# Second mixer's front: operands of small VectorE instructions moved to PSUM, and GpSimd's low parts of six strips made whole

## The chip, the cores and the metric

The kernel runs on one core of a Trainium2 chip, in one launch. The time is device microseconds of that core; the runs shown agree within 1.2 us. The engines are TensorE (PE; its weight loads are PEld in the profile), VectorE (DVE), ScalarE (ACT), GpSimd (POOL) and SyncE (SP), which issues the DMAs.

## What is computed

The reference is two small transformers in a row, on 256 tokens of width 1024, in float32: two layers of the first kind, then two of the second. The change lies in the second kind, `hybrid_layer`; here is its part that matters:

```python
h = rms_norm(x, ln_mix)
z = h @ w_in                                    # split into n_q, n_kc, ..., m_q, merge
q   = partial_rope(rms_norm(split_heads(q, H), q_norm), positions) * (dh ** -0.5)
k_s = partial_rope(rms_norm(split_heads(k_s, G), k_norm[1]), positions)
k_w = partial_rope(rms_norm(split_heads(k_w, G), k_norm[2]), positions)
...
k, v = jnp.split(rms_norm(mem, mem_norm) @ w_kv, 2, axis=-1)    # memory attention
k = rms_norm(split_heads(k, H), k_norm)
```

`partial_rope` turns the first 16 of a head's 64 values by the angles of the positions: `[x1*cos - x2*sin, x2*cos + x1*sin, rest]`. `rms_norm` divides by the root of the mean square. Behind the mixers of a layer stands an MLP; the first kind of layer has two gated MLPs around a mixer of its own.

## The kernel before

**The stream.** All big weights come as 616 pieces of 128 x 1024 float32, in the order of use, by SyncE's queue into a ring of 7 places. Each piece is multiplied to nearly float32 precision by three fast products. ScalarE rounds the piece (`round_piece`, L1350: `hi`), GpSimd subtracts that from the piece (`pool_program`, L563: `lo`, in the piece's own place), and TensorE multiplies `hi` with the high part of the activations, `lo` with the same, and `hi` with their low part (`product`, L590 to L592). A piece of a strip is 12 matmuls of 512 columns. ScalarE rounds a piece at most 4 ahead of TensorE, in a ring of 5, and waits for `used`, TensorE's count of pieces done.

**GpSimd** does a piece in one instruction in the MLPs and in four (`parts`) in the mixers. Which pieces are in a mixer is told by `in_mixer`. Ahead of a piece in four parts it also waits until its previous piece has ended.

**The second mixer** (`mix2`) works on strips of 512 columns, four pieces each, in the order `nk, nq, z3, mk, mq, mv, gqk, gv`, six of `merge`, `gr`, and then rows of the branches. TensorE puts strips by turns into PSUM banks 0, 1 and 2, 3; ahead of a strip it waits until the strip two before it has been taken out (`evicted`). VectorE takes out `nk`, `z3`, `mv`, `gv` and the merges, ScalarE `mk`, `mq`, `gqk`.

Between the pieces each engine does small steps; their order is written out by hand in `mix2_work`, the same list for all engines. Around the change VectorE's order is this:

- `memory_in` 2: variance and square root of the memory rows (`m_cells`, 2 columns); ScalarE makes a first guess by Ln and Exp, VectorE improves it in four instructions (`rsqrt`, L1857 to L1860).
- `prep` 1: sums of squares of the 24 heads' values (L2199) and their variance (`variance`, L1866), for which ScalarE then waits with its next guess, in front of its next rounding.
- `windows` 0 and 1 (L2183, L2189): windows of keys and values for the compression, from PSUM.
- the taking of `z3` out of PSUM (L2052).
- `prep` 2: square root of the heads (`cells24`, 24 columns; `rsqrt`), then the heads are scaled (L2205).
- `prep` 3: the rotation by the angles (`rotate`, L2163 to L2168), six instructions on 192 columns.
- `mem` 1 and 3: variance and square root of the memory keys (`k_cells`, 8 columns), then the keys are scaled (L2219). TensorE transposes them behind strip `mq` (L812).

All these small instructions have their operands in SBUF; only the windows and the taking read PSUM. Later `nsa_step` 0 (L2346 to L2350) begins the hidden layer of the compression, and `mem_unit` makes the scores of the memory attention (L2236, L2040), which TensorE transposes (L822). L2355 ends the hidden layer's gelu; TensorE waits for it at L1126.

`TURNED` is PSUM bank 6, which TensorE uses for transposes before and behind these steps.

Of the kernel before, what the change touches and what calls it, by code (L numbers as in the profile page):

```python
# [15 lines left out]
ALU = mybir.AluOpType  # L16
# [3 lines left out]
P = 128  # L20
# [270 lines left out]
class Views:  # L291


    def __init__(self, M):
# [3 lines left out]
        def cell(n):  # L298
            at[0] += n
            assert at[0] <= 500, at  # L300
            return small[:, at[0] - n:at[0]]
# [100 lines left out]
        self.tmp_v = self.hid[1][:, 0:64]  # L402
        self.mn16, self.sum16, self.inv16 = cell(16), cell(16), cell(16)
        self.cells24 = (cell(24), cell(24), cell(24))
        self.cells8 = (cell(8), cell(8), cell(8))
        self.m_cells = (cell(2), cell(2), cell(2))
        self.k_cells = (cell(8), cell(8), cell(8))
        self.c_cells = (cell(1), cell(1), cell(1))
        self.dests = {"nk": self.znq[:, :, 512:1024], "nq": self.znq[:, :, 0:512], "mq": self.mq, "z3": self.zz,
                      "gqk": self.gqk, "gv": self.gv, "mk": M.memkv[:, :, 0:512], "mv": M.memkv[:, :, 512:1024]}  # L410
# [130 lines left out]
def in_mixer(c):  # L541

    block, at = divmod(c, PIECES1) if c < L * PIECES1 else divmod(c - L * PIECES1, PIECES2)
    if c < L * PIECES1:
        return FFN_PIECES + 6 <= at < PIECES1 - FFN_PIECES - 4
    return 8 <= at < PIECES2 - 8 * MLP_STRIPS - 4


def pool_program(M, sem):
# [768 lines left out]
def act_program(M, V, sem, landed):  # L1318
# [10 lines left out]
    def own(instruction):  # L1329

        instruction.then_inc(sem["act"], 1)
        act.wait_ge(sem["act"], nxt("act"))
# [16 lines left out]
        used = slice(0, 2 * half_width(c))  # L1349
        act.activation(M.hi[:, slot_hi, used], M.raw[:, slot, used], ACT.Copy).then_inc(sem["hi"], 1)  # L1350

    def rsqrt(cells):

        v, t, y = cells
        act.wait_ge(sem["var"], nxt("var"))
        own(act.activation(t, v, ACT.Ln))
        act.activation(y, t, ACT.Exp, scale=-0.5).then_inc(sem["guess"], 1)
        return nxt("rstd")

# [229 lines left out]
    def mix2(layer, c0, rstd):  # L1589
# [12 lines left out]
        def mem_step(i):  # L1602
            if i == 0:
                act.wait_ge(sem["z_mk"], layer + 1)
                squares(M.memkv, V.head_sq, V.k_cells[0])
            elif i == 2:
                rsqrt(V.k_cells)
            elif i == 4:
                turn_qk("mem_k")
            elif i == 5:  # L1610
                act.wait_ge(sem["z_mq"], layer + 1)
                squares(V.mq, V.head_sq, V.cells8[0])
            elif i == 7:
                rsqrt(V.cells8)
            elif i == 8:
                act.wait_ge(sem["gains"], layer + 1)
                turn_qk("mem_q")
# [24 lines left out]
        for step in mix2_order():  # L1642
# [39 lines left out]
                                           scale=V.scale[:, m:m + 1])  # L1682
                    t.then_inc(sem["z_gr"], 1)
            elif what == "prep" and step[1] == 2:
                rsqrt(V.cells24)
            elif what == "mem":
                mem_step(step[1])
            elif what == "mem_unit":
                t = step[1]
                if t < 4:  # L1690
                    exponentials(t % 2, ((0, S), (S, S)))
                if 0 <= t - 2 < 4:
                    high_part(y_hi[:, Y2_TILE[2] + t - 2, :], psum[:, OUT, 0:S], ("o", nxt("o")), "y2hi")
            elif what == "gla":
                gla_step(step[1])
            elif what == "decay":
                hp, i = step[1:]
                if i in (1, 2):
                    e = V.decays[i - 1]
                    act.wait_ge(sem["diff"], nxt("diff"))  # L1700
                    own(act.activation(e, e, ACT.Abs))
                    act.activation(e, e, ACT.Exp, scale=-1.0 / 16).then_inc(sem["decay"], 1)
            elif what == "nsa":
                i = step[1]
                if i == 1:
                    a = V.hid[1]
                    act.wait_ge(sem["cdve"], 8 * layer + 2)
                    act.activation(a, a, ACT.Exp, scale=-2.0 * math.sqrt(2.0 / math.pi)).then_inc(sem["cact"], 1)
                elif i == 3:
                    rsqrt([a[0:32, :] for a in V.c_cells])  # L1710
                elif i == 5:
                    act.wait_ge(sem["gclip"], layer + 1)
                    act.activation(V.gates, V.gates, ACT.Exp, scale=-1.0).then_inc(sem["gexp"], 1)
                elif i == 6:
                    turn_qk("nsa", end=2)
                elif i == 7:
                    turn_qk("nsa", first=2)
            elif what == "nsa_unit":
                t = step[1]
                if t == 0:  # L1720
                    act.wait_ge(sem["cshift"], layer + 1)
                    act.activation(V.pc, V.pc, ACT.Exp, scale=-1.0).then_inc(sem["cexp"], 1)
                elif t % 2 and t < NSA_UNITS:
                    exponentials(1, SEG)
                    exponentials(0, SEG)
                if t % 2 == 0 and t >= 4:
                    o, j = nxt("o", 2), (t - 3) // 4
                    if t % 4 == 2:
                        col = S * (j % 2)
                        high_part(y_hi[:, Y2_TILE[0] + j, :], psum[:, OUT, col:col + S], ("o", o), "y2hi")  # L1730
            elif what == "rows":
                round_piece(piece[step] + AHEAD)
            elif what == "gate":
                b = step[1]
                if b == 2:
                    act.wait_ge(sem["z_merge"], 6 * layer + 6)
                for m in range(MT):
                    w = V.merge[:, m, b * D:b * D + D]
                    act.activation(w, w, ACT.Sigmoid).then_inc(sem["sigmoid"], 1)
                if b == 1:  # L1740
                    exp_and_ln()
            elif what == "last_branch":
                rest = last_rows(last_c, 2, 0, False)
                c = last_c + 2
                features(None, M.h_hi, (0, 1, 2, 3), rest)
                for i in range(4):
                    round_piece(c + i + AHEAD)
                rest = last_rows(c + 4, 4, 0, False)
                c += KD
# [80 lines left out]
def dve_program(M, V, sem):  # L1830
# [9 lines left out]
    def nxt(name, k=1):  # L1840
        n[name] += k
        return n[name]
# [10 lines left out]
    def rsqrt(cells):  # L1853

        v, t, y = cells
        dve.wait_ge(sem["guess"], nxt("guess"))
        own(dve.tensor_tensor(t, y, y, ALU.mult))  # L1857
        own(dve.tensor_tensor(t, t, v, ALU.mult))
        own(dve.tensor_scalar(t, t, -0.5, 1.5, ALU.mult, ALU.add))
        dve.tensor_tensor(y, y, t, ALU.mult).then_inc(sem["rstd"], 1)  # L1860
        return nxt("rstd")

    def variance(cells, width):
# [306 lines left out]
    def mix2(layer, c0, rstd):  # L2170
# [23 lines left out]
        def prep(i):  # L2194
            heads = V.znq[:, :, 0:768].rearrange("p m (h d) -> p m h d", d=64)
            if i == 1:
                dve.wait_ge(sem["nsk"], layer + 1)
                dve.wait_ge(sem["nsq"], MT * (layer + 1))
                own(dve.tensor_reduce(V.cells24[0], V.softf[:, 0:1536].rearrange("p (g d) -> p g d", d=64), AX.X,  # L2199
                                      ALU.add))  # L2200
                variance(V.cells24, 64)
            elif i == 2:
                dve.wait_ge(sem["rstd"], rsqrt(V.cells24))
                scales = V.cells24[2].rearrange("p (m h) -> p m h", m=MT)
                own(dve.tensor_tensor(heads, heads, scales.unsqueeze(3).broadcast_to((P, MT, 12, 64)), ALU.mult))  # L2205
            elif i == 3:
                cos, sin = (V.trig[:, f, 0:MT, :].unsqueeze(2).broadcast_to((P, MT, 12, 8)) for f in range(2))
                rotate(heads, cos, sin, [V.softf[:, 192 * i:192 * i + 192].rearrange("p (m h d) -> p m h d", m=MT, h=12)
                                         for i in range(4)]).then_inc(sem["rotated"], 1)

        def mem_step(i):
            if i == 1:
                dve.wait_ge(sem["ss"], nxt("ss"))
                variance(V.k_cells, P)
            elif i == 3:
                k3 = M.memkv[:, :, 0:512].rearrange("p m (h d) -> p m h d", h=4)
                dve.wait_ge(sem["rstd"], rsqrt(V.k_cells))
                scales = V.k_cells[2].rearrange("p (m h) -> p m h", m=MT)
                dve.tensor_tensor(k3, k3, scales.unsqueeze(3).broadcast_to((P, MT, 4, P)),  # L2219
                                  ALU.mult).then_inc(sem["mkey"], 1)  # L2220
            elif i == 6:
                dve.wait_ge(sem["ss"], nxt("ss"))
                variance(V.cells8, P)
            elif i == 7:
                done["mq"] = rsqrt(V.cells8)
# [566 lines left out]
```

## Time and profile before

| | us |
|---|---|
| median of 3 runs | 1915.97 (1914.88 to 1916.08) |
| the profiled execution | 1917.5 |
| its span, first to last instruction | 1915.8 |
| TensorE busy | 1901.5 (99%) |
| GpSimd busy | 1573.1 (82%) |
| VectorE busy | 1050.1 (55%) |
| ScalarE busy | 1040.3 (54%) |

TensorE's matmuls overlap, and the profile models their ends: a matmul of 512 columns is shown with 0.39 us, though the next one starts 0.23 us behind it. A wait of TensorE shorter than that overlap does not show as idle time, only as a larger distance of two starts. In rows of the timeline an idle time ahead of an instruction stands in brackets, with what ended it. The granted TensorE clock is full in all 40 slices. The two layers of the second kind begin near 980 us and 1440 us of the span; their fronts look alike.

### The profile page before, as it was taken

What the parts mean: (1) busy time and instruction counts of PE and PEld (TensorE: products, weight loads), DVE (VectorE), ACT (ScalarE), POOL (GpSimd) and SP (SyncE); (2) the same over time, 40 slices, a digit from 0 to 9 for tenths busy, and PEclk for the clock granted to TensorE, in tenths of its full rate; (3) what the DMA queues carried; (4) which work ended last, traced back from release to release, by engine and by line L of the source; (5) the groups of instructions that cost most, each with busy time, mean ns of one, the idle gap of its engine ahead of it and who ended that gap; (6) DMA issues with size and microseconds to landing.
All of it is one profiled execution on the core that took longest, in us unless ns stands there. A gap on an engine that the chain in (4) does not pass through costs nothing.

```text
span 1915.8 us, 26859 instructions
## 1 busy us (share of the span) xinstructions
PE 1901.5 (99%) x9404; PEld 1545.4 (81%) x9404; DVE 1050.1 (55%) x2655; ACT 1040.3 (54%) x1775; POOL 1573.1 (82%) x1160
## 2 busy tenths in 40 slices
PE   9999999999999999999999999999999999999999
PEld 7888777888888877788888877788888777788887
DVE  4768545544644745554455687547444677654553
ACT  6445666444744476654466444655446554565543
POOL 8888876988798877698879777779887968788986
PEclk9999999999999999999999999999999999999999
DMA  6665434555565543367556343456657433345654
GB/s 243 242 207 183 164 118 150 194 192 197 201 236 195 192 163 121 122 223 254 194 187 245 121 143 122 144 176 207 244 197 255 162 125 126 127 145 197 194 192 142
DMA packets 98337, 346.87 MB, mean 181 GB/s; under 512 B 13180, under 2 KB 13852, under 8 KB 97948
## 3 DMA queue, kind: packets, MB, share of 16 engines
q1 hardware_dynamic: 97628, 344.03, 52.5%
q8 instruction: 75, 1.23, 0.3%
q10 hardware_dynamic: 576, 1.14, 0.2%
q14 instruction: 58, 0.48, 0.1%
HBM read 344.08 MB, written 1.05 MB: 180 GB/s over the span
## 4 chain that ended last, share of the span: by engine, by line
PE 94%; POOL 2%; DVE 1%; ACT 1%; DMA 1%; issue 0%; SPq 0%; POOLq 0%; DVEq 0%; ACTq 0%
PE psum L590 28%; PE psum L592 28%; PE psum L591 28%; POOL lo L563 2%; PE psum L822 1%; PE psum L659 1%; PE psum L832 1%; PE psum L845 1%; PE psum L1057 1%; PE psum L812 1%; PE psum L868 0%; PE psum L909 0%; PE psum L1213 0%; DMA x<-in_x 0%; DMA raw<-in_stream 0%
## 5 line engine op out<-in xcount | busy, mean ns | idle before, releaser
L563 POOL TENSOR_TENSOR lo<-raw,hi 128x256 fp32r<-128x256 f32 (+2 forms) x1156 | 1572.9, 1385 | 329.7 <-ACT hi L1350 300.8
L1350 ACT ACTIVATE hi<-raw 128x1024 fp32r<-128x1024 f32 (+1 forms) x616 | 642.2, 1053 | 484.6 <-PE psum L592 457.9
L590 PE MATMUL psum<-hi,h_hi 128*128 128x512 f32 x1616 | 640.7, 396 | 2.8 <-POOL lo L563 1.9
L592 PE MATMUL psum<-hi,h_lo 128*128 128x512 f32 x1616 | 627.9, 389 | 0.0
L591 PE MATMUL psum<-lo,h_hi 128*128 128x512 f32 x1616 | 627.2, 388 | 0.0
L590 PEld LDWEIGHTS psum<-hi,h_hi 128*128 128x128 f32 x1616 | 304.0, 188 | 69.6 <-POOL lo L563 5.0
L592 PEld LDWEIGHTS psum<-hi,h_lo 128*128 128x128 f32 x1616 | 303.3, 188 | 63.8
L1990 DVE STREAM_TRANSPOSE psum<-big 32x128 f32<-32x128 f32 (+1 forms) x960 | 344.1, 358 | 14.2
L591 PEld LDWEIGHTS psum<-lo,h_hi 128*128 128x128 f32 x1616 | 303.8, 188 | 58.5
L590 PE MATMUL psum<-hi,y_hi 128*128 128x512 f32 x832 | 328.2, 394 | 0.0
L592 PE MATMUL psum<-hi,y_lo 128*128 128x512 f32 x832 | 324.3, 390 | 0.0
L591 PE MATMUL psum<-lo,y_hi 128*128 128x512 f32 x832 | 324.0, 389 | 0.0
L1999 DVE TENSOR_TENSOR y_lo<-psum,y_hi 128x512 fp32r<-128x512 f32 x76 | 51.0, 689 | 331.6 <-ACT y_hi L1473 331.3
L590 PEld LDWEIGHTS psum<-hi,y_hi 128*128 128x128 f32 x832 | 156.2, 188 | 35.4 <-issue 1.7
L592 PEld LDWEIGHTS psum<-hi,y_lo 128*128 128x128 f32 x832 | 156.1, 188 | 33.2
L591 PEld LDWEIGHTS psum<-lo,y_hi 128*128 128x128 f32 x832 | 156.3, 188 | 31.1
L1515 ACT ACTIVATE soft<-soft,small 128x128 f32<-128x128 f32 (+1 forms) x120 | 54.6, 456 | 131.2 <-DVE small L2029 109.1
L1978 DVE SCALAR_TENSOR_TENSOR big<-psum,small,big 128x256 f32<-128x256 f32 (+1 forms) x120 | 61.1, 550 | 88.2 <-ACT big L1463 88.2
L1463 ACT ACTIVATE big<-psum,small 128x256 f32<-128x256 f32 (+1 forms) x120 | 57.2, 527 | 54.3 <-PE psum L592 54.2
L1473 ACT ACTIVATE y_hi<-psum 128x512 fp32r<-128x512 f32 x76 | 42.7, 583 | 15.4 <-DVE psum L1990 15.4
L2048 DVE COPY soft<-psum 128x384 f32<-128x384 f32 (+2 forms) x68 | 35.4, 520 | 27.3 <-PE psum L822 27.3
L822 PE MATMUL psum<-consts,soft 128*128 128x128 f32 x188 | 34.4, 287 | 2.3 <-DVE soft L2040 2.3
(296 smaller groups left out, 1342.4 us busy)
## 6 DMA issues: line engine op xcount, KB each, us to landing
raw<-in_stream SPq DMA_DIRECT2D x608, 512.0 KB, 3.6
big<-in_w SPq DMA_DIRECT2D x14, 512.0 KB, 6.2
big<-in_post SPq DMA_DIRECT2D x6, 512.0 KB, 5.0
special<-in_b_merge SPq DMA_DIRECT2D x2, 1536.0 KB, 7.6
raw<-in_stream SPq DMA_DIRECT2D x8, 296.0 KB, 5.4
memkv<-in_mem SPq DMA_DIRECT2D x2, 1024.0 KB, 6.7
big<-in_band SPq DMA_DIRECT2D x2, 768.0 KB, 5.5
x<-in_x SPq DMA_DIRECT2D x2, 512.0 KB, 7.1
```

What stands on the lines that cost most here:

```text
L563: t = pool.tensor_tensor(M.lo[:, slot, w], M.raw[:, slot, w], f32(M.hi[:, slot_hi, w]), ALU.subtract)
L590: pe.matmul(out, lhs_hi, rhs_hi, start=start, stop=False)
L591: pe.matmul(out, lhs_hi, rhs_lo, start=False, stop=False)
L592: return pe.matmul(out, lhs_lo, rhs_hi, start=False, stop=stop)
L822: t = pe.transpose(psum[:, TURNED, i * P:i * P + P], soft[:, slot, 0, col:col + P], V.ident)
L1350: act.activation(M.hi[:, slot_hi, used], M.raw[:, slot, used], ACT.Copy).then_inc(sem["hi"], 1)
L1463: t = act.activation(act_s[:, m, :], psum[:, bank + m, 0:width], ACT.Silu if gated else ACT.Relu, scale=V.scale[:, m:m + 1])
L1473: act.activation(flat(y_hi[:, kt:kt + 2, :]), psum[:, bank + g, :], ACT.Copy).then_inc(sem["yhi"], 1)
L1515: t = act.activation(out, prob[:, w], ACT.Exp, scale=-1.0, bias=mn[:, i:i + 1], accum_out=total[:, i:i + 1])
L1978: t = dve.scalar_tensor_tensor(prod_s[:, m, :], psum[:, bank + m, col:col + width], V.scale[:, m:m + 1], act_s[:, m, :], ALU.mult, ALU.mult)
L1990: t = dve.transpose(dst[32 * b:32 * b + 32, :, :, 32 * a:32 * a + 32], src[32 * a:32 * a + 32, :, :, 32 * b:32 * b + 32])
L1999: dve.tensor_tensor(flat(y_lo[:, kt:kt + 2, :]), psum[:, bank + g, :], f32(flat(y_hi[:, kt:kt + 2, :])), ALU.subtract).then_inc(sem["ylo"], 1)
```

## The change

It has four parts.

- `in_mixer`: of the second mixer's pieces, numbers 8 to 23 of a layer (strips `z3` to `mv`) now count as outside, so GpSimd does them in one instruction each and without the wait for its own previous piece. Pieces 0 to 7 were whole already.
- Square roots of the heads and of the memory keys: ScalarE writes its guess twice, to SBUF and to PSUM bank 6, and VectorE improves it in three instructions (`spare_rsqrt`) that each have one operand in PSUM; the result lies in PSUM.
- The heads and the memory keys are scaled by that result.
- Rotation: the angles are copied to PSUM first (one more instruction, 48 columns), and two of the four intermediate products lie in PSUM.

The square root of the memory rows (`m_cells`) and the three variances are as before.

```diff
+        spare = M.psum[:, TURNED, :]
+        self.spare24 = (spare[:, 0:24], spare[:, 24:48])
+        self.turned_trig = spare[:, 48:96]
+        self.turned_tmps = [spare[:, 128 + 192 * i:320 + 192 * i] for i in range(2)]
...
+        self.k_spare = (spare[:, 0:8], spare[:, 8:16])
...
 def in_mixer(c):
...
-    return 8 <= at < PIECES2 - 8 * MLP_STRIPS - 4
+    return 24 <= at < PIECES2 - 8 * MLP_STRIPS - 4
...
     def rsqrt(cells, spare=None):                  # ScalarE
         v, t, y = cells
         act.wait_ge(sem["var"], nxt("var"))
         own(act.activation(t, v, ACT.Ln))
+        if spare:
+            act.activation(y, t, ACT.Exp, scale=-0.5)
+            y = spare[0]
         act.activation(y, t, ACT.Exp, scale=-0.5).then_inc(sem["guess"], 1)
...
+    def spare_rsqrt(cells, spare):                 # VectorE
+        v, y, (y2, t) = cells[0], cells[2], spare
+        dve.wait_ge(sem["guess"], nxt("guess"))
+        own(dve.tensor_tensor(t, y2, y, ALU.mult))
+        own(dve.scalar_tensor_tensor(t, t, -0.5, v, ALU.mult, ALU.mult))
+        dve.scalar_tensor_tensor(y2, t, 1.5, y, ALU.add, ALU.mult).then_inc(sem["rstd"], 1)
+        return nxt("rstd")
...
-                dve.wait_ge(sem["rstd"], rsqrt(V.cells24))
-                scales = V.cells24[2].rearrange("p (m h) -> p m h", m=MT)
+                dve.wait_ge(sem["rstd"], spare_rsqrt(V.cells24, V.spare24))
+                scales = V.spare24[0].rearrange("p (m h) -> p m h", m=MT)
...
+                own(dve.tensor_copy(V.turned_trig, V.trig_flat))
+                trig = V.turned_trig.rearrange("p (f m i) -> p f m i", f=2, m=3)
...
+                places = (V.turned_tmps[0], V.softf[:, 0:192], V.turned_tmps[1], V.softf[:, 192:384])
...
-                dve.wait_ge(sem["rstd"], rsqrt(V.k_cells))
-                scales = V.k_cells[2].rearrange("p (m h) -> p m h", m=MT)
+                dve.wait_ge(sem["rstd"], spare_rsqrt(V.k_cells, V.k_spare))
+                scales = V.k_spare[0].rearrange("p (m h) -> p m h", m=MT)
```

## Rows read from the trace of the kernel before

**Rows 1.** The page, part 1: engine, busy us (share of the span) xinstructions.
```profile
PE 1901.5 (99%) x9404; PEld 1545.4 (81%) x9404; DVE 1050.1 (55%) x2655; ACT 1040.3 (54%) x1775; POOL 1573.1 (82%) x1160
```
**Rows 2.** Waits of TensorE, whole run: us in total, times, longest us.
```profile
PE psum L822 <- DVE soft L2040: 2.3, 4, 0.8
PE psum L590 <- POOL lo L563: 1.9, 4, 0.8
...
PE psum L1126 <- DVE extra L2355: 0.7, 2, 0.3
```
**Rows 3.** Chain of waits, 1012 to 1045 us: start us, us, what.
```profile
1018.57 2.84 POOL lo L563 x4
...
1021.54 2.83 POOL lo L563 x4
...
1030.48 4.34 POOL lo L563 x4
```
**Rows 4.** Timeline of TensorE, 1031 to 1076 us: start us, us, instruction.
```profile
1031.23 0.39 PE L590 MATMUL psum<-hi,h_hi 128*128 128x512 f32 x1
...
1033.72 0.39 PE L592 MATMUL psum<-hi,h_lo 128*128 128x512 f32 x1
1034.87 0.50 PE L590 MATMUL psum<-hi,h_hi 128*128 128x512 f32 x1 [0.76 <-POOL lo L563]
...
1045.27 1.03 PE L812 MATMUL psum<-consts,memkv 128*128 128x128 f32 x8
...
1075.51 0.66 PE L822 MATMUL psum<-consts,soft 128*128 128x128 f32 x4 [0.77 <-DVE soft L2040]
```
**Rows 5.** Groups by shape, GpSimd: line, instruction xcount | busy us, mean ns.
```profile
L563 POOL TENSOR_TENSOR lo<-raw,hi 128x1024 fp32r<-128x1024 f32 x436 | 1039.6, 2409 | 200.2 <-ACT hi L1350 199.5
L563 POOL TENSOR_TENSOR lo<-raw,hi 128x256 fp32r<-128x256 f32 x688 | 518.3, 777 | 128.4 <-ACT hi L1350 101.4
```
**Rows 6.** Chain of waits, the MLP behind: whole pieces in a row.
```profile
1260.09 7.12 POOL lo L563 x3
```
**Rows 7.** Timeline of GpSimd, from 1018 us.
```profile
1018.57 53.44 POOL L563 TENSOR_TENSOR lo<-raw,hi 128x256 fp32r<-128x256 f32 x68 [0.71 <-ACT hi L1350]
```
**Rows 8.** Timeline of VectorE, 998 to 1042 us.
```profile
998.65 0.16 DVE L1857 TENSOR_TENSOR small<-small 128x2 f32<-128x2 f32 x1 [0.51 <-ACT small L1357]
...
1018.85 0.47 DVE L1857 TENSOR_TENSOR small<-small 128x2 f32<-128x2 f32 x1 [0.97 <-ACT small L1357]
...
1021.34 1.74 DVE L2199 TENSOR_REDUCE small<-soft 128x24 f32<-128x1536 f32 x1
1023.11 0.59 DVE L1866 TENSOR_SCALAR small<-small 128x24 f32<-128x24 f32 x1
...
1024.27 1.94 DVE L2189 TENSOR_TENSOR big<-psum,special 64x120 f32<-64x120 f32 x8
...
1028.87 0.96 DVE L2052 TENSOR_SCALAR big<-psum,small 128x296 f32<-128x296 f32 x2
...
1041.39 1.23 DVE L2219 TENSOR_TENSOR memkv<-memkv,small 128x1024 f32<-128x1024 f32 x1
```
**Rows 9.** Groups by line, VectorE: tiny instructions in the first MLP, beside whole pieces.
```profile
L2562 DVE TENSOR_SCALAR extra<-small 128x8 f32<-128x8 f32 x3 | 7.0, 2406 | 0.0
```
**Rows 10.** Timeline of ScalarE, 1018 to 1067 us.
```profile
1018.72 1.99 ACT L1350 ACTIVATE hi<-raw 128x1024 fp32r<-128x1024 f32 x2
1023.74 0.22 ACT L1356 ACTIVATE small<-small 128x24 f32<-128x24 f32 x1 [3.02 <-DVE small L1866]
...
1024.12 3.00 ACT L1350 ACTIVATE hi<-raw 128x1024 fp32r<-128x1024 f32 x3
...
1066.35 1.05 ACT L1350 ACTIVATE hi<-raw 128x1024 fp32r<-128x1024 f32 x1
```
**Rows 11.** Timeline of VectorE, 1069 to 1072 us.
```profile
1069.16 0.82 DVE L2347 TENSOR_TENSOR extra<-extra 128x128 f32<-128x128 f32 x1
...
1071.44 0.65 DVE L2350 TENSOR_SCALAR extra<-extra 128x128 f32<-128x128 f32 x1
```

More of the change, by code:

```diff
@@ L1350, in round_piece, with rsqrt @@
         act.activation(M.hi[:, slot_hi, used], M.raw[:, slot, used], ACT.Copy).then_inc(sem["hi"], 1)
-    def rsqrt(cells):
+    def rsqrt(cells, spare=None):
         v, t, y = cells
@@ L1606, in mem_step @@
             elif i == 2:
-                rsqrt(V.k_cells)
+                rsqrt(V.k_cells, V.k_spare)
             elif i == 4:
@@ L1684, in mix2 @@
             elif what == "prep" and step[1] == 2:
-                rsqrt(V.cells24)
+                rsqrt(V.cells24, V.spare24)
             elif what == "mem":
@@ L2202, in prep @@
             elif i == 2:
-                dve.wait_ge(sem["rstd"], rsqrt(V.cells24))
-                scales = V.cells24[2].rearrange("p (m h) -> p m h", m=MT)
+                dve.wait_ge(sem["rstd"], spare_rsqrt(V.cells24, V.spare24))
+                scales = V.spare24[0].rearrange("p (m h) -> p m h", m=MT)
                 own(dve.tensor_tensor(heads, heads, scales.unsqueeze(3).broadcast_to((P, MT, 12, 64)), ALU.mult))
             elif i == 3:
-                cos, sin = (V.trig[:, f, 0:MT, :].unsqueeze(2).broadcast_to((P, MT, 12, 8)) for f in range(2))
-                rotate(heads, cos, sin, [V.softf[:, 192 * i:192 * i + 192].rearrange("p (m h d) -> p m h d", m=MT, h=12)
-                                         for i in range(4)]).then_inc(sem["rotated"], 1)
+                own(dve.tensor_copy(V.turned_trig, V.trig_flat))
+                trig = V.turned_trig.rearrange("p (f m i) -> p f m i", f=2, m=3)
+                cos, sin = (trig[:, f, 0:MT, :].unsqueeze(2).broadcast_to((P, MT, 12, 8)) for f in range(2))
+                places = (V.turned_tmps[0], V.softf[:, 0:192], V.turned_tmps[1], V.softf[:, 192:384])
+                rotate(heads, cos, sin, [a.rearrange("p (m h d) -> p m h d", m=MT, h=12)
+                                         for a in places]).then_inc(sem["rotated"], 1)
         def mem_step(i):
```

## The prediction, made before the result was known

> **What bounds the kernel now.** Read the page's first part first: TensorE is busy 1901.5 us of the 1915.8 us span [rows 1]. The profiled execution took 1917.5 us in all, 1.7 us more than its span and 1.5 us more than the median of the runs, 1915.97 us; I work out a difference from the trace and add it to the median. With TensorE at 99%, only its waits can be saved, so the list of what TensorE waited for comes next. It is short: in the whole run it idled 1.9 us for GpSimd's low parts, 2.3 us for VectorE's normalised memory scores (L2040), 0.7 us for VectorE's L2355 [rows 2]. Nothing that frees GpSimd can give back much more than the first two.
>
> Third, the chain of waits at the front of the second mixer shows where the GpSimd wait lies. From 1018.57 the chain runs through one low part after another, 2.84 us each, and through one of 4.34 us that starts at 1030.48 [rows 3]. TensorE's own timeline has the price: the third strip behind (mq) starts at 1031.23, its first piece ends its issue at 1033.72, and the next matmul, due 0.23 us later at 1033.95, starts at 1034.87 [rows 4]. That is 0.92 us, and the list has such a wait in each of the two layers [rows 2]. This is what the change goes for: two times 0.92 us.
>
> **The change, GpSimd's side.** A piece whole is 2.41 us; a quarter is 0.78 us on average [rows 5], and with the wait between pieces they go by at 2.97 us a piece (1018.57 to 1021.54 [rows 3]). Whole pieces that follow without a wait take 7.12 us for three [rows 6]. So a piece is 0.6 us shorter, and 16 pieces of each layer are changed. GpSimd now works without a break from 1018.57 for 53.44 us [rows 7]; that backlog goes away.
>
> **VectorE's side: what is not moved to PSUM.** Here I find the cost. The rows show how a small VectorE instruction fares beside GpSimd. With GpSimd idle the first step of a square root takes 0.16 us; at 1018.85, beside quarters, the same line takes 0.47 us, and the four steps need 2.5 us until the reduction behind them starts at 1021.34 [rows 8]. Beside whole pieces, three tiny instructions on SBUF took 2.41 us each, 7.0 us in all [rows 9]: each waits until the GpSimd instruction that runs has ended, and then one such instruction gets through per GpSimd instruction. The edits give a PSUM operand to the square roots of the heads and of the memory keys, to the scaling and to the rotation. They leave the memory rows' square root (four instructions from 1018.85) and the variance of the heads as they are, and these now stand beside whole pieces.
>
> Step by step, in layer 0. GpSimd's piece starts at 1018.57, 0.28 us ahead of VectorE's first step, because ScalarE rounds that piece just before it makes the guess; the two next pieces are rounded by 1020.71 (1018.72 and 1.99) [rows 10]. So three whole pieces run to 1018.57 + 7.12 = 1025.69, and VectorE's first three steps end with them. The fourth finds GpSimd idle, because ScalarE's next rounding stands behind its wait for the heads' variance, 3.02 us long now [rows 10]: with the 0.03 us between two instructions of VectorE (1023.08 to 1023.11) it ends at 1025.69 + 0.03 + 0.16 = 1025.88. The reduction (1.74 us) starts just ahead of that end, as before, and ends at 1027.59; the variance, free now, at 1027.78. Before, it ended at 1023.11 + 0.59 = 1023.70 [rows 8]. VectorE is 4.08 us late.
>
> What stands behind it. The windows' instructions and the copy of strip z3 out of PSUM follow in VectorE's order, and read PSUM, so they keep their durations. The copy ended at 1028.87 + 0.96 = 1029.83 [rows 8] and would end at 1033.91. TensorE needs it: strip mq goes into the bank of z3 and waits for that copy. It had 1.40 us to spare at 1031.23 [rows 4]; now it starts at about 1033.96, 2.73 us late. ScalarE's late rounding is the smaller wait: rounding began at 1024.12, 0.42 us behind the variance [rows 10], and with one more exponential (0.1 us) begins near 1028.3; with 1.0 us for it and 2.4 us for the low part, that piece is ready near 1031.8. The old 0.92 us is gone, since the next low part is ready 2.4 us later, at 1034.2, and TensorE comes to it at 1033.96 + 2.7. Net: 2.73 - 0.92 = 1.81 us **lost** per layer.
>
> Then the gains. The heads' scaling and the rotation no longer wait and no longer hold GpSimd (the piece of 4.34 us). No row shows a 24-column instruction from and to PSUM. Its floor is the 0.16 us of SBUF alone, its ceiling a whole piece, 2.41 us; I take 0.24 us, from the eight instructions with one PSUM and one SBUF input that took 1.94 us beside busy quarters [rows 8]. The copy of the angles into PSUM has the same ends. With 0.24 us, key scaling ends near 1041.3 instead of 1042.62 (1041.39 and 1.23 [rows 8]), and TensorE's transposes of it come at 1045.27 [rows 4] plus 1.8: 5.8 us of cover, so one or two of these that waited would still cost nothing, eleven would not.
>
> The Trainium skill, SBUF — State Buffer, "A bandwidth-pool intuition that's wrong", says that the side blocked at the shared port goes on about 115 ns after the other has ended. The three instructions of rows 9 need 7.0 us where three GpSimd pieces need 7.1, so here I see no such extra; by the page the three blocked steps would cost 0.35 us more a layer, an estimate, and the sum 0.7 us more.
>
> Second gain, later: the last piece of the backlog was rounded by 1066.35 + 1.05 = 1067.40 [rows 10] and its quarters ended at 1018.57 + 53.44 = 1072.01 [rows 7]; with the backlog gone they end 2.9 us after the rounding, at 1070.3, counted against TensorE, 1.7 us earlier. The first steps of the compression's hidden layer on VectorE, four from 1069.16 to 1071.44 + 0.65 = 1072.09, take 0.64 to 0.82 us each beside quarters [rows 11]; the last two would be free and take 0.2 to 0.3 us: 1.2 us. TensorE's wait at 1075.51 for the scores made behind them, 0.77 us [rows 4], is covered by that: 0.8 us back a layer. But VectorE's next scores come from TensorE, which gains less than VectorE does there, so L2355, later on the same engine, gains less than TensorE: its wait, 0.3 us now [rows 2], grows. The ends are 0 and 0.8 us; I take that wait once more, 0.3 us.
>
> Transfers: none is moved, SP's queue waits for TensorE as before and shifts with it. Later pieces stay quartered.
>
> **Sum**: 1.81 - 0.8 + 0.3 = 1.3 us a layer, 2.6 us for two: 1915.97 + 2.6 = 1918.6 us. About 0.2% (3.8 us) is what a measurement can tell, so that is no change, on its slow side.
>
> **Rivals.** *The late gain fails* (slower). If GpSimd still holds quarters beside the four steps at 1069, nothing comes back: 2 x (1.81 + 0.3) = 4.2 us, 1920.2 us. It decides from a lead of GpSimd below 1.2 us there. Against it: 16 pieces save 0.6 us each; for it: the lead is capped by ScalarE's rounding, which waits for TensorE.
>
> *The memory rows' steps slip through* (faster). If only the first step waits for a whole piece, VectorE is late by 0.3 us or so, within the 1.40 us to spare; both waits go, 0.92 + 0.8 a layer, with L2355's share up to 2.1: 1911.8 to 1912.5 us. Against it are rows 9, and GpSimd's pieces standing rounded.
>
> *PSUM operands don't exempt.* Then eleven instructions wait 2.41 us each, 26 us against 5.8 us of cover: some 20 us a layer, 1956 us. Against it are the 0.24 us beside quarters. The Trainium skill, SBUF — State Buffer, "Who interferes with whom", speaks against it too: a VectorE instruction with at most one SBUF input, outside the two-port modes, doesn't contend with GpSimd; the trace shows this for PSUM sources, and no row for small PSUM destinations.
>
> **Chances**: forecast 0.66, late gain fails 0.22, slip through 0.08, no exemption 0.03. The likeliest's own range is 1917.0 to 1920.2 us: 0.3 us a layer for VectorE's lag and 0.5 us for what comes back, either way. The range reaches to the slower rival and half-way to the faster: 1915.0 to 1920.8 us. The bound of 0.2% lies at 1919.8 us above, so 0.05 of the forecast and 0.15 of the first rival are slower; of the second 0.05 are beyond the bound below. Faster by over 0.2%: 0.06; within: 0.71; slower: 0.23.
>
> **What would show it.** Right: three steps of L1857 to L1859 of 2.1 to 2.4 us after 1018.85; TensorE waiting some 2.4 us for L2052 before strip mq; no wait for GpSimd at the piece behind; the wait for L2040 gone; scaling and rotation in PSUM at 0.2 to 0.35 us a small step, GpSimd's pieces at 2.4 us throughout. Wrong: steps at 1018.85 of 0.2 to 0.7 us, or TensorE starting strip mq at its old place.

## The result, and the profile after

The change makes the kernel a little slower: 1922.17 us is the median (6 executions, 1919.46 to 1922.73) against 1914.91 us for the kernel before on the same chip (1914.78 to 1916.08). The ratio is 1.0030, 95% interval 1.0019 to 1.0040, or 5.7 us (the two medians alone lie 7.3 us apart). The forecast was 2.6 us, 1918.6 us in all, and no change beyond 0.2%: the interval starts just inside the 0.2%, and the time lies above the upper end of the range, 1920.8 us. The profiled execution took 1922.61 us with a span of 1920.9 us, 5.1 us above the span before. The traced execution of the kernel before took 1917.5 us, 1.4 us more than the slowest of these six, so a loss read from trace against trace may come out too small.

The page's first part, after, answers to [rows 1]:

```profile
PE 1904.2 (99%) x9404; PEld 1547.7 (81%) x9404; DVE 1044.5 (54%) x2653; ACT 1039.9 (54%) x1779; POOL 1553.7 (81%) x1064
```

Every engine but TensorE has as much to do as before or less (GpSimd 19 us less in 96 fewer instructions), and the kernel is slower. TensorE is busy 2.7 us longer with the same 9404 matmuls: that is a first hint of a slower clock. Its waits in the whole run, after (us in total, times, longest), answer to [rows 2]:

```profile
PE psum L595 <- DVE big L2069: 5.1, 2, 2.6
...
PE psum L1131 <- DVE extra L2375: 1.1, 2, 0.5
...
PE psum L827 <- DVE soft L2057: 0.8, 2, 0.4
...
PE psum L595 <- POOL lo L568: 0.5, 2, 0.2
```

The wait for GpSimd is gone at the second mixer's front, the wait for the scores is shorter by 1.5 us, and a new wait, 2.6 us in each layer, stands first: TensorE waits for the copy of strip z3 out of PSUM (L2069, formerly L2052). VectorE's timeline, after, shows where that copy was held up; it answers to [rows 8]:

```profile
1018.66 2.13 DVE L1865 TENSOR_TENSOR small<-small 128x2 f32<-128x2 f32 x1 [1.11 <-ACT small L1365]
1020.83 2.33 DVE L1866 TENSOR_TENSOR small<-small 128x2 f32<-128x2 f32 x1
1023.20 2.32 DVE L1867 TENSOR_SCALAR small<-small 128x2 f32<-128x2 f32 x1
1025.55 0.16 DVE L1868 TENSOR_TENSOR small<-small 128x2 f32<-128x2 f32 x1
1025.63 1.75 DVE L2216 TENSOR_REDUCE small<-soft 128x24 f32<-128x1536 f32 x1
1027.42 0.18 DVE L1883 TENSOR_SCALAR small<-small 128x24 f32<-128x24 f32 x1
...
1032.76 0.96 DVE L2069 TENSOR_SCALAR big<-psum,small 128x296 f32<-128x296 f32 x2
1033.64 0.18 DVE L1875 TENSOR_TENSOR psum<-psum,small 128x24 f32<-128x24 f32 x1
...
1036.09 0.21 DVE L2224 COPY psum<-extra 128x48 f32<-128x48 f32 x1
1036.34 0.36 DVE L2180 TENSOR_TENSOR psum<-big,psum 128x192 f32<-128x192 f32 x1
```

Three instructions on two columns take 2.13 to 2.33 us each. GpSimd's timeline in the same stretch, after, shows what they wait for, three whole pieces in a row:

```profile
1018.38 7.11 POOL L568 TENSOR_TENSOR lo<-raw,hi 128x1024 fp32r<-128x1024 f32 x3 [1.65 <-ACT hi L1355]
```

They end at 1018.38 + 7.11 = 1025.49, and the third of VectorE's steps at 1025.52; the fourth, free, takes 0.16 us. TensorE's timeline, after, answers to [rows 4]:

```profile
1033.78 0.50 PE L595 MATMUL psum<-hi,h_hi 128*128 128x512 f32 x1 [2.57 <-DVE big L2069]
1034.12 0.39 PE L596 MATMUL psum<-lo,h_hi 128*128 128x512 f32 x1
...
1035.83 0.63 PE L596 MATMUL psum<-lo,h_hi 128*128 128x512 f32 x1
1036.25 0.63 PE L597 MATMUL psum<-hi,h_lo 128*128 128x512 f32 x1
...
1037.96 0.63 PE L595 MATMUL psum<-hi,h_hi 128*128 128x512 f32 x1
...
1077.81 0.60 PE L827 MATMUL psum<-consts,soft 128*128 128x128 f32 x4
```

Strip mq starts 2.55 us late (1033.78 against 1031.23). The fifth piece's first matmul (1037.96) waits for nothing any more. But between them the matmuls follow each other every 0.43 us, not every 0.23 us. The windows of TensorE, after, say why (columns: window, us, busy us and instructions of PE, PEld, DVE, ACT, POOL, then the granted clock, the DMA share and GB/s):

```profile
1035.10:1038.50 3.40, 3.40 (x10) 2.63 (x9) 3.30 (x9) 1.74 (x6) 3.40 (x2) 0.50 0.00 0
1038.50:1042.00 3.50, 3.50 (x32) 2.43 (x34) 1.93 (x5) 1.96 (x5) 3.50 (x3) 1.00 0.46 150
1499.30:1502.70 3.40, 3.40 (x9) 2.64 (x10) 3.23 (x9) 2.67 (x13) 3.40 (x3) 0.50 0.01 2
```

For 3.4 us in each layer the granted clock is 0.50, that is 1.2 GHz instead of 2.4 GHz, behind an idle of 2.57 us in the first layer (from 1.3 us behind its end on) and of 2.58 us in the second (at once). The first layer's starts from 1034.12 to 1038.91 are 14 steps in 4.79 us; at 0.227 us they would take 3.18. So the slow stretch costs 1.6 us, the second layer's 1.7 us (nine steps from 1499.16 to 1502.91, against 2.04 us). No wait shows it: the engine is busy.

Start against start, matmul by matmul, the first layer loses 2.55 us at strip mq, some 1.6 us in the slow stretch and 0.1 us in the restart, gets 0.9 us back at the old wait for GpSimd and 0.8 to 0.9 us at the scores, and ends at +2.5 us. The second ends at +5.1 us.

### The profile page after: what moved, and what is told of

It is laid out like the page before. It is cut to its first block, busy times and chain, and to the rows that moved or that the text cites. A ratio compares the mean times of both kernels' runs of the same rounds, so it can differ in the third digit from the quotient of the medians.

```text
span 1920.9 us, 26733 instructions
## 1 busy us (share of the span) xinstructions
PE 1904.2 (99%) x9404; PEld 1547.7 (81%) x9404; DVE 1044.5 (54%) x2653; ACT 1039.9 (54%) x1779; POOL 1553.7 (81%) x1064
## 4 chain that ended last, share of the span: by engine, by line
PE 95%; DVE 2%; ACT 1%; POOL 1%; issue 0%; DMA 0%; SPq 0%; ACTq 0%; DVEq 0%
PE psum L595 29%; PE psum L597 28%; PE psum L596 28%; PE psum L827 1%; PE psum L664 1%; PE psum L837 1%; PE psum L850 1%; PE psum L1062 1%; POOL lo L568 1%; PE psum L817 1%; PE psum L873 0%; PE psum L914 0%; PE psum L1218 0%; PE psum L1018 0%; DVE big L2206 0%
## 5 line engine op out<-in xcount | busy, mean ns | idle before, releaser
L568 POOL TENSOR_TENSOR lo<-raw,hi 128x256 fp32r<-128x256 f32 (+1 forms) x1060 | 1553.5, 1488 | 354.2 <-ACT hi L1355 330.7
```

The costliest lines, as they stand in the source:

```text
L568: t = pool.tensor_tensor(M.lo[:, slot, w], M.raw[:, slot, w], f32(M.hi[:, slot_hi, w]), ALU.subtract)
```

## The experiments

The theory: (a) the memory rows' root, left on SBUF, waits three whole pieces and carries strip z3's copy past the point at which TensorE needs it; (b) the idle time that follows lets TensorE's clock fall, and that is the part the forecast lacked. The rivals: the PSUM operands themselves cost, the whole pieces gain nothing in any case, the slow clock has nothing to do with the idle.

**PSUM operands alone.**

```diff
-    return 24 <= at < PIECES2 - 8 * MLP_STRIPS - 4
+    return 8 <= at < PIECES2 - 8 * MLP_STRIPS - 4
```

> Only the PSUM operands of the change; the pieces of the six strips stay in quarters. Theory (the loss is VectorE's memory-row square root and the heads' variance waiting at the shared port for whole pieces, which makes the copy of strip z3 late): VectorE is not late, TensorE starts strip mq on time; GpSimd's piece of 4.34 us falls to 2.84 us because the heads' scaling no longer holds it, so the old wait of 0.92 us goes too, and with it most of the later 0.8 us: 1.5 to 1.8 us a layer, 3.0 to 3.6 us below the kernel before, ratio 0.998. No drop of TensorE's granted clock in the two mixer fronts. Rival (the whole pieces are what frees the path, PSUM operands cost VectorE time): within 0.5 us of the kernel before, the wait for GpSimd near 1034 us still there. Second rival (the PSUM operands themselves make VectorE late): slower than before, by 2 us or more.

Measured: 1913.36 us (11 executions), ratio to before 0.9989 [0.9980, 0.9998]. TensorE has one wait left between 990 and 1100 us, and VectorE's steps, in this kernel's timeline, take what they took before:

```profile
1017.36 0.47 DVE L1865 TENSOR_TENSOR small<-small 128x2 f32<-128x2 f32 x1 [0.93 <-ACT small L1365]
...
1027.39 0.96 DVE L2069 TENSOR_SCALAR big<-psum,small 128x296 f32<-128x296 f32 x2
```

So the PSUM operands are a gain, 2.1 us by the ratio, and the loss comes from the whole pieces. The ratio is short of the 3.0 to 3.6 us expected; the two traces lie 3.8 us apart behind the program's start, but the one of the kernel before is that of a long execution.

**Whole pieces alone.** The kernel before with the line that the first experiment took back:

```diff
-    return 8 <= at < PIECES2 - 8 * MLP_STRIPS - 4
+    return 24 <= at < PIECES2 - 8 * MLP_STRIPS - 4
```

> Only the whole pieces of the change; all VectorE operands stay in SBUF. Theory: the same late copy of z3 as with the whole change (TensorE waits 2.5 us before strip mq, clock drop behind it), and in addition eleven instructions of the heads' square root, scaling and rotation and the four of the keys' square root wait for a GpSimd piece each, up to 2.4 us, less where GpSimd stands idle: the keys' scaling is late and TensorE waits for it at its transposes; 5 to 20 us a layer, 1925 to 1955 us. Rival (VectorE instructions hardly wait, the PSUM edits were not needed): no longer than the whole change, 1918 to 1922 us.

Measured, one execution: 1925.72 us, a span 3.2 us above that of the change. The direction is right, the size at the low end of what was expected: matmul by matmul against the kernel before, the first layer loses 3.4 us, less than the 5 us expected at least, and the second 5.2 us. TensorE's waits in this kernel:

```profile
PE psum L590 <- DVE big L2052: 5.1, 2, 2.6
PE psum L812 <- DVE memkv L2219: 3.2, 2, 2.4
```

VectorE's timeline in this kernel shows the heads' root blocked three times and the scaling once, and the rotation behind them no more:

```profile
1033.76 2.31 DVE L1858 TENSOR_TENSOR small<-small 128x24 f32<-128x24 f32 x1
...
1038.42 2.33 DVE L1860 TENSOR_TENSOR small<-small 128x24 f32<-128x24 f32 x1
1040.79 3.88 DVE L2205 TENSOR_TENSOR big<-big,small 128x1536 f32<-128x1536 f32 x1
1044.70 0.36 DVE L2163 TENSOR_TENSOR soft<-big,extra 128x192 f32<-128x192 f32 x1
```

And GpSimd's:

```profile
1028.97 14.08 POOL L563 TENSOR_TENSOR lo<-raw,hi 128x1024 fp32r<-128x1024 f32 x6 [3.64 <-ACT hi L1350]
1048.12 8.62 POOL L563 TENSOR_TENSOR lo<-raw,hi 128x1024 fp32r<-128x1024 f32 x6 [5.07 <-ACT hi L1350]
```

The late VectorE holds up the whole front, GpSimd runs out of rounded pieces at 1043.05 and idles for 5.07 us, and the rotation behind runs free, 0.36 us a step. Here the blocking limits itself.

This one execution also tells of TensorE's clock three times. In the first layer TensorE idled 2.55 us ahead of strip mq, and from 1034.89 on its matmuls follow at 0.43 us. In the second layer it idled 2.56 us ahead of the same strip and 2.40 us ahead of the transposes of the memory keys. First the two rows of its timeline, then its windows behind each:

```profile
1499.77 0.50 PE L590 MATMUL psum<-hi,h_hi 128*128 128x512 f32 x1 [2.56 <-DVE big L2052]
...
1515.43 1.33 PE L812 MATMUL psum<-consts,memkv 128*128 128x128 f32 x8 [2.40 <-DVE memkv L2219]
```

```profile
1499.80:1503.20 3.40, 3.40 (x15) 2.82 (x16) 3.33 (x3) 2.99 (x14) 3.40 (x3) 1.00 0.10 42
1516.20:1519.50 3.30, 3.30 (x10) 2.67 (x9) 0.00 (x0) 2.24 (x4) 3.30 (x2) 0.50 0.00 0
```

The clock stayed full behind the 2.56 us and fell behind the 2.40 us, so the length of the idle does not decide alone.

**The memory rows' root in PSUM as well.** The change, with the root that it left out done the same way; its result goes back to SBUF:

```diff
-                    m_rstd = rsqrt(V.m_cells)
+                    m_rstd = rsqrt(V.m_cells, V.m_spare)
...
-                    m_rstd = root(V.m_cells, D)
+                    variance(V.m_cells, D)
+                    m_rstd = spare_rsqrt(V.m_cells, V.m_spare, V.m_cells[2])
```

> The whole change, and the memory rows' square root gets PSUM operands too (guess twice, three instructions, result in SBUF). Theory: these steps take 0.2 us each beside whole pieces; the heads' variance still waits for one whole piece and ends near 1023.2 us of the span, as before the change (1023.7). The copy of z3 is on time, no wait before strip mq, no clock drop, no wait for GpSimd behind it: 1.5 to 1.9 us a layer below the kernel before, 3.0 to 3.8 us in all, ratio 0.998; against the change some 7 to 10 us. Rival (TensorE's wait before strip mq comes from ScalarE's late rounding or the doubled guess, not from VectorE's steps): TensorE still waits over 1 us there and the time stays above the kernel before.

Measured: 1913.43 us (11 executions), ratio 0.9987 [0.9979, 0.9996]. VectorE's timeline in this kernel:

```profile
1018.41 0.17 DVE L1876 TENSOR_TENSOR psum<-psum,small 128x2 f32<-128x2 f32 x1 [1.17 <-ACT psum L1366]
...
1020.68 2.18 DVE L1884 TENSOR_SCALAR small<-small 128x24 f32<-128x24 f32 x1
...
1028.03 0.96 DVE L2070 TENSOR_SCALAR big<-psum,small 128x296 f32<-128x296 f32 x2
```

This is (a) shown: with three steps exempted, the new wait and the slow stretch both go. The heads' variance, still on SBUF, now waits for a whole piece (2.18 us), which the cover takes. By its interval this kernel lies below the old one, by some 0.1%, as do the first experiment's and the last one's. It equals the first experiment's within the intervals: no run shows that the whole pieces add anything to what the PSUM operands give.

**The idle time filled.** The change, with twelve matmuls into a bank that is free there, ahead of TensorE's wait for z3:

```diff
+                if (i, j) == (4, 0):
+                    for _ in range(12):
+                        pe.matmul(psum[:, OUT, :], h_hi[:, 0, 0:P], flat(h_hi[:, 0:2, :]), start=True, stop=True)
```

> The whole change, and TensorE multiplies 12 pieces of 512 columns of the activations into a free PSUM bank ahead of the wait for z3 (2.7 us of work whose result nobody reads). Theory (the half-speed stretch of 3.4 us behind that wait is owed to TensorE having stood idle): no stretch at half of the granted clock near 1035 and 1499 us, everything else as in the change: 3.2 to 3.4 us less than executions of the change that show both stretches (1922.2 us), so 1918.5 to 1919.6 us, ratio to before 1.002. Rival (the clock falls for another reason, by the load of the stretch or by chance): the stretches stay in most executions, 1922 us. Second rival: the filler itself delays strip mq by more than the wait, over 1922 us.

Measured: 1919.11 us (11 executions, 1917.73 to 1920.76), ratio 1.0016 [1.0007, 1.0025], or 3.1 us above before. TensorE's windows in this kernel, from the start of strip mq on in each layer:

```profile
1032.30:1038.50 6.20, 6.20 (x37) 4.75 (x40) 5.34 (x15) 4.74 (x20) 6.20 (x4) 1.00 0.29 94
1496.00:1502.70 6.70, 6.70 (x45) 5.08 (x48) 5.80 (x16) 5.23 (x19) 6.70 (x4) 1.00 0.22 82
```

Strip mq waits as long as before, but TensorE is busy meanwhile, and the clock stays at 1.00. The time saved is that of the slow stretches, 0.14% or 2.7 us by the two ratios (intervals overlap at the edge), 3.5 us by the two traces behind the program's start, where the one of the change was 1.38 us behind already. That is (b) for this execution; whether it is more than chance is settled by all executions, below.

**Half of the idle time filled.** Six such matmuls instead of twelve.

> The change with six idle-filling matmuls instead of twelve: TensorE idles about 1.2 us instead of 2.6 ahead of strip mq. The six leave nothing in the output. If any idle time of this size costs the half-speed stretch, the time is that of the change (ratio to before 1.003); if idle time of 1.2 us still passes at full clock, it is that of the twelve (1.0016, some 1919 us), with granted clock 1.00 in 1035 to 1039. I expect the second, since a wait of 0.76 us in the kernel before passed at full clock.

Measured: 1918.06 us (11 executions, 1917.77 to 1919.38), ratio 1.0013 [1.0004, 1.0022]. In this kernel TensorE's timeline has the rest of the wait, and the windows the clock behind it:

```profile
1032.35 0.50 PE L595 MATMUL psum<-hi,h_hi 128*128 128x512 f32 x1 [1.19 <-DVE big L2072]
```

```profile
1032.30:1038.50 6.20, 6.16 (x36) 4.74 (x40) 5.34 (x15) 4.73 (x20) 6.20 (x4) 1.00 0.29 94
1496.00:1502.70 6.70, 6.63 (x44) 5.06 (x48) 5.78 (x17) 5.24 (x20) 6.70 (x4) 1.00 0.25 87
```

An idle of 1.19 us, in the second layer 1.21 us, leaves the clock alone, as the 0.76 us of [rows 4] did. With the clock kept, the change costs 2.5 us by this ratio, against a forecast of 2.6.

**The change once more**, for how often the clock falls.

> The change itself, more executions. Theory (each half-speed stretch of TensorE, 3.4 us long, costs some 1.5 us): executions fall into groups by their mean granted clock, one stretch more lowering it by 3.4 x 0.5 / 1920 = 0.0009; those at 0.999 end near 1919.5 us, those at 0.997 to 0.998 near 1922 us, as in the six executions so far. Rival (the groups come from elsewhere, a transfer at the start, say): times of 1919 and 1922 us both with clocks spread from 0.997 to 0.999. The median stays within 1919.4 to 1922.8 us.

Measured: 1921.89 us (9 executions, 1919.20 to 1922.24), ratio 1.0027 [1.0018, 1.0037]. The groups are only half as clear as expected: one of 1919.2 us has a mean clock of 0.999, those at 0.997 and 0.998 took 1920.9 to 1922.2 us, but two of 1921.9 us stand at 0.999 and one of 1920.78 us at 1.0. The last is the profiled one. Its timeline and its windows of TensorE:

```profile
1035.08 0.50 PE L595 MATMUL psum<-hi,h_hi 128*128 128x512 f32 x1 [2.56 <-DVE big L2069]
1035.42 0.40 PE L596 MATMUL psum<-lo,h_hi 128*128 128x512 f32 x1
1035.66 0.39 PE L597 MATMUL psum<-hi,h_lo 128*128 128x512 f32 x1
```

```profile
1035.10:1038.50 3.40, 3.40 (x15) 2.83 (x16) 3.23 (x9) 3.11 (x16) 3.40 (x3) 1.00 0.04 14
1499.00:1502.40 3.40, 3.40 (x15) 2.80 (x16) 3.23 (x9) 3.08 (x14) 3.40 (x3) 1.00 0.00 0
```

The idle is the same, 2.56 us and in the second layer 2.57 us, and the matmuls behind it follow at 0.23 us: here the clock did not fall, in either layer. This execution was 1.15 us behind that of before already at 13 us, from slow matmuls in the program's first microseconds, where executions of either kernel differ. From there to the end it lost 3.29 - 1.15 = 2.14 us, the change without its clock term. So the idle of 2.6 us may lower the clock and need not; what decides it is open.

That the idle is what the falls hang on is seen over all executions. The mean granted clock is 0.998 or less in 9 of the 15 of the change, in none of the 22 with the idle filled wholly or in half, and in none of the 67 of the kernel before that ran beside the experiments. On one chip, the 11 executions with six matmuls took 1917.8 to 1919.4 us, and 8 of the 9 of the change 1920.8 to 1922.2 us.

**z3 taken ahead of the second window.** The change, with `windows[1]` one place later in VectorE's order:

```diff
-        "z3": ([prep[0]], [memory_in[2]], [prep[1], windows[0], windows[1]], [prep[2]]),
+        "z3": ([prep[0]], [memory_in[2]], [prep[1], windows[0]], [windows[1], prep[2]]),
```

> The whole change, with one step moved in the written order: the second window of the compression comes behind the taking of strip z3 instead of ahead of it, on all engines. VectorE's wait for whole pieces stays (it is 4 us late at the heads' variance), but the copy of z3 has 2.4 us less in front of it. Theory (what costs is that TensorE's strip mq waits for the copy of z3, and the half-speed stretch of 3.4 us is owed to the length of that idle time): the copy ends near 1031.2 us of the span, TensorE then waits for the low part of the first mq piece until 1031.7, 0.6 us; no half-speed stretch; 3.5 to 3.8 us a layer less than an execution of the change with two such stretches, so 1914 to 1916 us, ratio to before 0.998 to 1.000. Rival (another wait ends just behind it: rounding, the memory keys, the moved window): TensorE still waits 2 us or more before or behind strip mq, 1919 us or more. Second rival (any idle time of that place brings the half-speed stretch): 1917 to 1919 us with the stretches there.

Measured: 1914.94 us (11 executions), ratio 0.9993 [0.9984, 1.0002]. The first row is VectorE's, the second TensorE's, of this kernel's timelines:

```profile
1028.74 0.96 DVE L2069 TENSOR_SCALAR big<-psum,small 128x296 f32<-128x296 f32 x2
```

```profile
1030.41 0.47 PE L595 MATMUL psum<-hi,h_hi 128*128 128x512 f32 x1 [0.56 <-POOL lo L568]
```

VectorE's lag is unchanged (its three steps still take 2.12 to 2.33 us), only its order is: the copy comes 2.6 us sooner behind the heads' variance, and TensorE idles 0.56 us, for the low part that ScalarE rounded late. The clock stays at 1.00. A second way of taking the idle away, without added work, gives the same answer.

**Quarters, and PSUM for the heads' root and scaling only.** The change with the quarters back, and with the rotation and the memory keys as they were:

```diff
-    return 24 <= at < PIECES2 - 8 * MLP_STRIPS - 4
+    return 8 <= at < PIECES2 - 8 * MLP_STRIPS - 4
...
-                places = (V.turned_tmps[0], V.softf[:, 0:192], V.turned_tmps[1], V.softf[:, 192:384])
+                places = [V.softf[:, 192 * i:192 * i + 192] for i in range(4)]
...
-                dve.wait_ge(sem["rstd"], spare_rsqrt(V.k_cells, V.k_spare))
+                dve.wait_ge(sem["rstd"], rsqrt(V.k_cells))
```

> Quarters everywhere as before the change, and of the PSUM edits only the heads' square root and scaling; rotation and memory keys stay in SBUF. Theory (the old wait of 0.92 us is owed to one quarter of GpSimd that the scaling of 1536 columns held up, its 2.24 us; the rotation and the key scaling only feed the backlog that makes the later scores late): GpSimd's piece at 1030.5 takes 2.84 us, the wait of 0.92 us is gone in both layers; the wait for the scores (0.77 us before) falls by 0.2 to 0.5 us only; 1.0 to 1.3 us a layer below the kernel before, 2.0 to 2.6 us in all, between the kernel before and the run with all PSUM edits, ratio 0.9988 to 0.9992. Rival (the old wait was owed to the quarters' slower pace altogether): the wait stays at 0.5 us or more, within 1 us of the kernel before.

Measured: 1914.30 us (11 executions), ratio 0.9990 [0.9981, 0.9999]. VectorE's timeline in this kernel has the scaling, free:

```profile
1029.84 1.75 DVE L2222 TENSOR_TENSOR big<-big,psum 128x1536 f32<-128x1536 f32 x1
```

The old wait is gone in both layers, so the heads' root and scaling were its cause (the two were not tried apart; the scaling is the one of them that stood beside the piece of 4.34 us [rows 3]). The rotation's and the keys' operands are not needed for that; they shorten the backlog further and with it the wait for the scores (0.5 us here in the first layer, none with all the PSUM operands).

## Why the prediction was right in mechanism and wrong in size

**VectorE's lag** was right: heads' variance at 1027.60 instead of 1023.70, so 3.9 us late (forecast 4.08). The Trainium skill, SBUF — State Buffer, "A bandwidth-pool intuition that's wrong", states some 115 ns more behind the release, of the opposite case, GpSimd held up by VectorE; here the third step ended 0.03 us behind the third piece, so the trace does not show it for a VectorE step behind GpSimd.

**Strip mq** started at 1033.78 (forecast 1033.96), behind the wait that was named. **The old wait** went, 0.9 us. **The late gain** came: the hidden layer's last two steps took 0.29 and 0.23 us (forecast 0.2 to 0.3), 0.8 to 0.9 us back at the scores; the rival that denied it fell. The forecast's 1.2 us for these steps does not follow from its parts: 0.72 + 0.65 us less 0.4 to 0.6 is 0.8 to 1.0; the trace has 1.1 us, because the first of the four was shorter as well, 0.56 instead of 0.82 us. The 0.8 us of the sum does not hang on it. **L2375's wait** grew by 0.2 us a layer (forecast 0.3). **The small PSUM steps** took 0.17 to 0.19 us and the copy of the angles 0.21 (taken: 0.24), so the rival that PSUM operands don't exempt fell too, and with the 2.13 to 2.33 us of the three steps the one in which they slip through.

**The step that failed** is the sum: "1.81 - 0.8 + 0.3 = 1.3 us a layer" prices an idle TensorE at its idle time alone. The 2.57 us of idle had a second price, 1.6 us of half clock per layer in the profiled execution, 3.3 us for both; 2.6 + 3.3 = 5.9 against 5.1 between the traces and 5.7 by the ratio; against the traces the rest is small terms that came out a little better, the lag by 0.2 us a layer. By the Trainium skill, TensorE: Matmul & The Clock Gate, "Wait — 56ns, not 53.3ns?", a 512-column matmul starts 426.7 ns after the one before at the lower level; the trace agrees (0.43 us). The kernel before has no idle as long as this in its second mixers, and a clock of 1.00 there; but its trace had the sign at the program's start, which the forecast did not read. First TensorE's timeline, then its windows, of the kernel before:

```profile
7.48 1.71 PE L703 MATMUL psum<-consts,x 128*128 128x128 f32 x8 [2.38 <-DMA x<-in_x]
```

```profile
7.70:11.10 3.40, 3.40 (x16) 3.22 (x15) 0.99 (x3) 2.52 (x5) 1.17 (x2) 0.51 1.04 419
```

A wait of 2.38 us there, the longest in TensorE's list of waits but left out of [rows 2], and 3.4 us at half clock behind it. The 9 in the page's row of the clock means 90% or more: the first slice of 48 us has a mean of 0.96, so the clock was not full in all 40 slices. The sign is a weak one, though. Two more traces have it at the same place, behind 2.25 and 2.29 us; in the other seven the matmuls were slow ahead of the wait already (0.21 us apart, against 0.11 us in the kernel before), and they are slow behind waits of 1.36, 1.50 and 1.82 us and fast behind 1.59, 1.67 and 1.81 us. With the forecast's own idle of 2.73 us beside it, that would have been a rival of some 1.6 us a layer. Without the term the forecast stands: with half of the idle filled the ratio is 1.0013, 2.5 us, and the execution without slow stretches lost 2.14 us.

What the runs leave open is why the clock fell behind 2.57 us in one execution and not behind 2.56 us in another, and in one and the same execution behind 2.55 and 2.40 us and not behind 2.56 us.

## What to carry to other kernels

When a shared port makes small instructions wait, move all of those that stand beside the longer blocker, or leave the blocker short: three two-column instructions left behind cost more than the shorter work of 16 pieces saved. Where an edit puts a new wait on a TensorE that runs without breaks, look in the trace for the longest wait that it already has and for the clock behind it, and price the slower matmuls as a rival of their own.

## What the runs showed of the hardware

- One tiny VectorE instruction on SBUF gets through per GpSimd instruction, and does not lengthen it: three pieces took 7.11 us with three such steps between them, 7.12 us without [rows 6].
- The scaling with two SBUF inputs took 3.88 us beside whole pieces, 2.26 us of it until the piece that ran had ended at 1043.05; with one of them in PSUM it took 1.75 us, as long as the reduction, which has one input.
- TensorE went to half clock behind 2.57 and 2.58 us of idle in the second mixer (the two layers of one execution of the change) and behind 2.55 and 2.40 us (whole pieces alone). It stayed at full clock behind 2.56 and 2.57 us (another execution of the change), behind 2.56 us (whole pieces alone), and behind 0.56, 0.76 and 1.19 us. Twelve or six matmuls in the idle kept it full in the traced executions.
- The recorded clock can say 1.00 where the matmuls are slow. In the second profile of the change the program's start has this row in TensorE's timeline, and the next in its windows:

```profile
10.38 2.05 PE L722 MATMUL psum<-hi,h_hi 128*128 128x512 f32 x4
```

```profile
7.70:11.10 3.40, 3.40 (x16) 3.30 (x16) 0.88 (x2) 2.40 (x5) 0.95 (x2) 1.00 1.04 419
```

With half of the idle filled the same four matmuls took 1.17 us. The spacing of the matmuls is the surer sign, so the clock of 1.00 behind 2.56 us was read together with the spacing of 0.23 us.
